# Triangle inverse by doubling in an RWKV-7 layer: 32 instead of 64 moving columns in each product, as a strided view

## The chip, the cores and the metric

One Trainium2 chip, of which the kernel uses one core. The metric is the device time of one execution in microseconds (us). The engines are TensorE (PE in the rows, its weight loads PEld), VectorE (DVE), ScalarE (ACT), GpSimd (POOL) and SyncE (SP, which issues the DMAs).

## What is computed

A trunk of two residual layers on 256 frames of 2048 features, in float32. Layer 0 mixes tokens by forgetting attention, layer 1 by RWKV-7 time mixing, and each is followed by a gated ConvFFN (5632 hidden features); each part has RMS norms before and after, and shift, scale and gate from a conditioning vector (adaLN). The change is in the RWKV-7 part, whose heart is this recurrence over the frames, for 32 heads of 64 features:

```python
def step(state, inp):
    r_t, w_t, k_t, v_t, kk_t, a_t = inp
    sa = jnp.einsum('bhvk,bhk->bhv', state, kk_t)
    state = (state * w_t[:, :, None, :]
             - sa[..., None] * (kk_t * a_t)[:, :, None, :]
             + v_t[..., None] * k_t[:, :, None, :])
    y = jnp.einsum('bhvk,bhk->bhv', state, r_t)
    return state, y
```

The kernel computes it in four chunks of 64 frames. Within a chunk the values sa solve a triangular system of 64x64 with a unit diagonal, so each head and chunk needs the inverse of such a matrix.

## The kernel before

**The whole.** Activations lie feature-major in SBUF. The big weight matrices are streamed in pieces of 512 KB by SP; ScalarE rounds each piece to fp32r (`whi`, L752), VectorE forms the rest (`wlo`, L1161), and TensorE multiplies (L1783 in `slab`, L1799 and L1802 in `paired_slab`). This fills nearly the whole time before and after the stage of the change.

**The chunk laps.** The RWKV recurrence runs in `chunk_laps`: 8 laps of 2 tiles, each tile 128 partitions that hold two heads of 64 features, so 4 heads x 4 chunks = 16 matrices a lap. `chunk_laps` issues lap 0 straight, laps 1 to 6 in a hardware loop of two laps, and then lap 7 and a last half lap. Every engine has its own `chunk_lap` with the order of its work written out by hand; semaphores named in `pr_pe`, `pr_a`, `pr_v` (preparation), `sc_*` (the recurrence) and `hd_*` (the head of the next lap) tie them together. A lap does three things at once: `prep`, the matrices of its own two tiles; `turn`, the recurrence over the four chunks of the two tiles before; and `ahead`, the LoRA products, decays and norms of the two tiles after. Beside these TensorE multiplies the adaLN weights of layer 1 by the conditioning vector (`gemv`, L2028, and `adaln_sum`, L1816, whose matmuls have one moving column).

**The inverse by doubling.** `ut[q]` holds, for each head (`h`, half of the partitions), tile `p` and chunk `c`, the inverse so far twice: index 0 upper, index 1 the transpose, lower. `lnm` holds the triangle to be inverted. `masked` and the step `tb` set level 0. Then for n = 1 to 5 (`LEVELS` = 6), with blocks of 2^n columns:

- `z_mm(n)` on TensorE: for both tiles 8 matmuls, Z = lnm^T ut0, 64 moving columns, into PSUM bank 0 or 1. It waits for `ut` of the level before.
- `z_out(n)` on ScalarE: copies Z from PSUM to `zsb` (L1098), 128x256, once per tile.
- `u_mm(n)` on TensorE: for both tiles and each matrix ut1^T zsb (upper) and, below the last level, zsb^T ut1 (lower), 64 moving columns each, into banks 2 and 3. It waits for ScalarE's copy.
- `doubled(n, p)` on VectorE: writes the product into `ut` where the level's mask is one (`copy_predicated`, L1678; L1674 at the last level).

The mask of level n keeps, in the upper half, only columns whose block number (column // 2^n) is odd, and in the lower half only those with an even one, as `shape_constants` says:

```python
lower = (h // m == q // m + 1) & ((q // m) % 2 == 0)
upper = (q // m == h // m + 1) & ((h // m) % 2 == 0)
```

**The order around it.** On TensorE the pairs lie between other work: Z1, the group norm's sum (`wide`), U1, the variance sum (`compact`), Z2, `spread_out`, the LoRA products of the next lap (`loras`), U2, `adaln_sum`, Z3, `gemv`, U3, the norms of kk (`compact`), `gemv`, Z4, `kk_spread`, `gemv`, U4, `bonuses`, `gemv`, Z5, `adaln_sum`, U5. All small matmuls go through `small_mm`, so the profile has them under L1979, and they are told apart by their tiles (a row names the output, the moving and the stationary operand in this order). `zsb` is not initialised before; the VectorE steps that come first in the stage (L1538 to L1550) end in the semaphore step `pone`, for which all engines wait before lap 0.

Of the kernel before, what the change touches and what calls it, by code (L numbers as in the profile page):

```python
# [33 lines left out]
ACT = mybir.ActivationFunctionType  # L34
# [3 lines left out]
P = 128  # L38
D = 2048
S = 256  # L40
# [8 lines left out]
HD = 64  # L49
# [25 lines left out]
LEVELS = 6  # L75
# [136 lines left out]
def trunk(nc, a, out):  # L212
# [20 lines left out]
    with ctx:  # L233
# [20 lines left out]
        def take(region, name, shape, dt=F32):  # L254

            region[0] = (region[0] + 31) // 32 * 32
            t, region[0] = at(name, region[0], shape, dt)
            assert region[0] <= region[1], (name, region)
            return t
# [16 lines left out]
        hka = take(small, "hka", [P, KT])  # L276
        hw0 = take(small, "hw0", [P, 2, KT])
# [73 lines left out]
        zsb = take(r1, "zsb", [P, 2, CH, HD])  # L351
        lnm = take(r1, "lnm", [P, 2, CH, HD])
        pcum = take(r1, "pcum", [P, 2, CH, HD + 1])
        csum = take(r1, "csum", [P, 2 * CH * HD])
        keep = take(r1, "keep", [P, 2 * CH * HD])
# [3 lines left out]
        ut = [take(r2, f"ut{q}", [P, 2, CH, 2, HD]) for q in range(2)]  # L359
# [13 lines left out]
        cst = take(r1, "cst", [P, KT, 32])  # L373
# [11 lines left out]
        ps = [duo[b // 2][:, b % 2, :] for b in range(4)]  # L385
# [20 lines left out]
        def steps(name, names, first=""):  # L406
            return Steps(sem(name), names, first)
# [14 lines left out]
                     v=steps(f"out{n}_v", "gain rinv t0 t1 x0 t2 x1 t3 x2 x3"))  # L422
                for n in range(4)]
# [11 lines left out]
                   z=steps(f"up{n}_z", "zero")) for n in range(2)]  # L435
# [13 lines left out]
                      + " ".join(f"z{n}p0 z{n}p1 u{n}p0 u{n}p1" for n in range(1, LEVELS)))  # L449
        pr_a = steps("pr_a", "vt bt kt " + " ".join(f"z{n}p{p}" for n in range(1, LEVELS) for p in range(2)))  # L450
        pr_v = steps("pr_v", "ub0 arb0 lk0 ub1 arb1 lk1 ln tb "
                     + " ".join(f"u{n}p{p}" for n in range(1, LEVELS) for p in range(2)), "hka nka hw0 one keep cz cst pone")
        sc_pe = steps("sc_pe", " ".join(f"rhs{c} sa{c} m{c} y{c}" for c in range(CH - 1)) + f" rhs{CH - 1} sa{CH - 1} "
                      f"y{CH - 1} mean var vx")
        sc_a = steps("sc_a", " ".join(f"rhs{c} sa{c}" for c in range(CH)) + " y sqy sd hi")
# [21 lines left out]
        def flat(t):  # L477
            return t[:, :, :].rearrange("p a s -> p (a s)")
# [42 lines left out]
        def waited(engine):  # L521

            engine.nop(nofuse=True)

        heads = (slice(0, HD), slice(HD, P))

        def chunk_laps(engine, head, lap):


            n = ph_chunk.iters  # L530
            head(0, 0)
            lap(0, 0, turn=False)
            with engine.Fori(0, n // 2 - 1) as j:
                lap(j * 2 + 1, 1)
                lap(j * 2 + 2, 0)
            lap(n - 1, 1, ahead=False)
            lap(n, 0, prep=False, ahead=False)
# [206 lines left out]
        def _(sc):  # L744
# [307 lines left out]
            def sigmoids(i):  # L1052

                t0 = i * 2
                sc.wait_ge(*hd_pe.at("lora", i))
                for b, nm in enumerate(("sw", "sa")):
                    for p in range(2):
                        sc.activation(sig[:, b, p, :], ps[4 + b][:, p * S:p * S + S], ACT.Tanh,
                                      bias=hw0[:, b, ds(t0 + p, 1)], scale=0.5).then_inc(*hd_a.inc(f"{nm}{p}"))
# [18 lines left out]
            def chunk_lap(i, q, prep=True, turn=True, ahead=True):  # L1078
                n_ = i - 1

                def out(name, bank):

                    if turn:
                        sc.wait_ge(*sc_pe.at(name, n_))
                        sc.activation((rhs_s if name[0] == "r" else sa)[:, :, :].rearrange("p a s -> p (a s)"),
                                      bank[:, 0:2 * HD], ACT.Copy).then_inc(*sc_a.inc(name))

                def tokens_out(name, dst, b):
                    if prep:
                        sc.wait_ge(*pr_pe.at(f"{name}tok", i))  # L1090
                        sc.activation(dst[q][:, :, :, :].rearrange("p a c s -> p (a c s)"), ps[b][:, :],
                                      ACT.Copy).then_inc(*pr_a.inc(f"{name}t"))

                def z_out(n):
                    if prep:
                        for p in range(2):
                            sc.wait_ge(*pr_pe.at(f"z{n}p{p}", i))
                            sc.activation(zsb[:, p, :, :].rearrange("p c s -> p (c s)"), ps[p][:, 0:S],  # L1098
                                          ACT.Copy).then_inc(*pr_a.inc(f"z{n}p{p}"))

                def gemv_result(u):

                    if prep:
                        sc.wait_ge(gemv_used, i * (KT // 2) + 4 * (u + 1))
                        sc.activation(mfin[:, 0:512], ps[7][:, :], ACT.Copy).then_inc(gemv_out, 1)

                tokens_out("v", vtok, 1)
                out("rhs0", ps[4])
                tokens_out("b", btok, 2)
                out("sa0", ps[5])  # L1110
                tokens_out("k", ktok, 3)
                for c in range(1, CH):
                    out(f"rhs{c}", ps[4])
                    out(f"sa{c}", ps[5])
                if turn:
                    sc.wait_ge(*sc_pe.at(f"y{CH - 1}", n_))
                    sc.activation(flat(ysb), ps[6][:, :], ACT.Copy).then_inc(*sc_a.inc("y"))
                z_out(1)
                if turn:
                    sc.wait_ge(*sc_v.at("yc", n_))  # L1120
                    sc.activation(sqy[:, :, :], yc[:, :, :], ACT.Square).then_inc(*sc_a.inc("sqy"))
                    sc.wait_ge(*sc_pe.at("var", n_))
                    sc.activation(sd8[:, :], ps[5][:, 0:8], ACT.Sqrt, bias=eps[1], scale=1.0 / HD).then_inc(
                        *sc_a.inc("sd"))
                gemv_result(0)
                z_out(2)
                if ahead:
                    sigmoids(i + 1)
                z_out(3)
                if ahead:  # L1130
                    norms(i + 1, 1 - q, turn)
                z_out(4)
                if turn:
                    sc.wait_ge(*sc_v.at("o", n_))
                    sc.activation(act[:, ds(n_ * 2, 2), 0, :], yc[:, :, :], ACT.Copy).then_inc(*sc_a.inc("hi"))
                gemv_result(1)
                z_out(5)
# [17 lines left out]
        def _(v):  # L1155
# [390 lines left out]
            v.memset(cst[:, :, :], 0.0).then_inc(*pr_v.inc("cz"))  # L1546
            v.wait_ge(*pr_v.at("cz"))
            v.tensor_copy(cst[:, :, 0], cact[:, :]).then_inc(*pr_v.inc("cst"))
            v.memset(pcum[:, :, :, 0:1], 1.0).then_inc(*pr_v.inc("pone"))
            v.nop().then_inc(*sc_v.inc("first"))  # L1550

# [209 lines left out]
        def _(pe):  # L1761
# [216 lines left out]
            def small_mm(dst, lhs, rhs, start=True, stop=True):  # L1978
                return pe.matmul(dst, lhs, rhs, start=start, stop=stop, skip_group_check=True)  # L1979
# [74 lines left out]
            def chunk_lap(i, q, prep=True, turn=True, ahead=True):  # L2054
# [73 lines left out]
                def z_mm(n):  # L2128
                    if not prep:
                        return  # L2130
                    for p in range(2):
                        pe.wait_ge(*(pr_v.at("tb", i) if n == 1 else pr_v.at(f"u{n - 1}p{p}", i)))
                        waited(pe)
                        for c in range(CH):
                            for h in heads:
                                last_ = small_mm(ps[p][h, c * HD:(c + 1) * HD], lnm[h, p, c, :],
                                                 ut[q][h, p, c, 0, :])
                        last_.then_inc(*c_.inc(f"z{n}p{p}"))

                def u_mm(n):  # L2140
                    if not prep:
                        return
                    for p in range(2):
                        pe.wait_ge(*pr_a.at(f"z{n}p{p}", i))
                        waited(pe)
                        for c in range(CH):
                            for h in heads:
                                last_ = small_mm(ps[2 + p][h, c * P:c * P + HD], ut[q][h, p, c, 1, :], zsb[h, p, c, :])
                                if n < LEVELS - 1:
                                    last_ = small_mm(ps[2 + p][h, c * P + HD:(c + 1) * P], zsb[h, p, c, :],  # L2150
                                                     ut[q][h, p, c, 1, :])
                        last_.then_inc(*c_.inc(f"u{n}p{p}"))

                if prep:
# [43 lines left out]
                if prep:  # L2198
                    gemv(i, 0, 3)
                z_mm(1)  # L2200
                if turn:
                    pe.wait_ge(*sc_a.at("y", n_))
# [75 lines left out]
```

## Time and profile before

| | |
|---|---|
| Median of 3 runs | 3188.09 us (3187.14 to 3192.75) |
| The profiled execution | 3189.45 us, span from first to last instruction 3187.7 us |
| Mean granted TensorE clock | 0.948 |
| TensorE busy | 2888.0 us, 91% of the span |
| VectorE / ScalarE / GpSimd busy | 62% / 46% / 4% |
| Stage of the chunk laps | about 1790 to 2276 us |

The span is one execution as the hardware profiler recorded it. Busy time counts an engine's own instructions; a busy TensorE may still wait inside its pipeline. An fp32 matmul of the source shows as two records, each with a weight load. PEclk is the clock granted to TensorE as a share of full speed (2.4 GHz); 0.50 is 1.2 GHz.

### The profile page before, as it was taken

The page shows a single profiled execution, that of the slowest core. Times are in us where ns is not written, and L with a number is a line of the kernel's source. Part 1 is how long each engine was busy: PE and PEld are TensorE (multiplying, and loading weights), DVE is VectorE, ACT ScalarE, POOL GpSimd, SP SyncE. Part 2 cuts the span into 40 slices and gives each one's busy share as a digit, 9 for nine tenths or more (in the row PEclk, how much of TensorE's full clock was granted, in tenths as well). Part 3 has the DMA queues.
Part 4 walks back from the last instruction along what each step waited for, and adds up shares of the span by engine and source line. Part 5 has one row for each costly group of instructions (what it writes and reads, how often), then busy time and mean ns, then how long its engine had stood idle before and what let it go on. Part 6 is the DMA issues. An engine that isn't in the chain of part 4 may idle for free.

```text
span 3187.7 us, 63222 instructions
## 1 busy us (share of the span) xinstructions
PE 2888.0 (91%) x24254; PEld 2598.9 (82%) x24254; DVE 1970.8 (62%) x2557; ACT 1474.7 (46%) x2011; POOL 136.2 (4%) x160
## 2 busy tenths in 40 slices
PE   2399999899999999985999798989789999999998
PEld 2399999888888899984888677767687888889998
DVE  6877777876666666678564344444337666665434
ACT  0133333466666643348554232322236666665333
POOL 0000000100000000000000221211000000000000
PEclk8599989999999999997999899999799999999999
DMA  8787877756666578872655454444444666655553
GB/s 297 259 279 266 290 262 264 268 170 192 188 191 188 185 241 290 274 238 69 189 178 178 136 172 142 151 159 160 128 144 152 185 186 185 188 184 175 183 172 126
DMA packets 506155, 628.09 MB, mean 197 GB/s; under 512 B 26392, under 2 KB 434824, under 8 KB 505736
## 3 DMA queue, kind: packets, MB, share of 16 engines
q1 hardware_dynamic: 501952, 622.62, 60.6%
q10 hardware_dynamic: 4040, 3.07, 0.3%
q8 instruction: 131, 2.15, 0.3%
q14 instruction: 32, 0.26, 0.0%
HBM read 623.50 MB, written 2.10 MB: 196 GB/s over the span
## 4 chain that ended last, share of the span: by engine, by line
PE 76%; DVE 10%; DMA 7%; ACT 3%; issue 3%; ACTq 0%; DVEq 0%; SPq 0%
PE ps L1799 26%; PE ps L1783 21%; PE ps L1802 13%; PE ps L1979 9%; DMA raw<-in_ffn_w_out 4%; DVE macc L1182 3%; DVE wlo L1161 2%; PE ps L2028 2%; ACT whi L752 1%; PE ps L1825 1%; PE ps L1816 1%; DMA raw<-in_mod_w 1%; DVE mx L1490 1%; PE ps L1889 1%; DMA raw<-in_fox_w_in 1%
## 5 line engine op out<-in xcount | busy, mean ns | idle before, releaser
L1161 DVE TENSOR_TENSOR wlo<-raw,whi 128x1024 fp32r<-128x1024 f32 x792 | 966.6, 1228 | 721.5 <-ACT whi L752 720.5
L752 ACT ACTIVATE whi<-raw 128x1024 fp32r<-128x1024 f32 x792 | 833.0, 1059 | 939.2 <-PE ps L1802 312.9
L1799 PE MATMUL ps<-xs,whi 128*128 128x512 f32 x3328 | 1172.1, 397 | 18.7 <-DVE xs L1245 10.9
L1802 PE MATMUL ps<-xs,wlo 128*128 128x256 f32 x3328 | 935.5, 281 | 0.0
L1799 PEld LDWEIGHTS ps<-xs,whi 128*128 128x128 f32 x3328 | 627.4, 189 | 168.1 <-issue 11.6
L1783 PE MATMUL ps<-act,whi 128*128 128x256 f32 x3840 | 708.5, 287 | 38.6 <-DVE wlo L1161 38.2
L1783 PEld LDWEIGHTS ps<-act,whi 128*128 128x128 f32 x3840 | 608.3, 195 | 45.7 <-DVE wlo L1161 44.9
L1802 PEld LDWEIGHTS ps<-xs,wlo 128*128 128x128 f32 x3328 | 631.9, 190 | 0.0
L1783 PE MATMUL ps<-act,wlo 128*128 128x256 f32 x1920 | 548.7, 286 | 0.0
L1783 PEld LDWEIGHTS ps<-act,wlo 128*128 128x128 f32 x1920 | 374.2, 195 | 0.0
L1182 DVE SCALAR_TENSOR_TENSOR macc<-raw,cact,macc 128x1024 f32<-128x1024 f32 (+1 forms) x252 | 293.0, 1163 | 9.0 <-DMA raw<-in_mod_w 4.2
L1783 PE MATMUL ps<-xs,whi 128*128 128x256 f32 x1024 | 201.2, 299 | 9.2 <-DVE xs L1245 5.7
L1783 PEld LDWEIGHTS ps<-xs,whi 128*128 128x128 f32 x1024 | 172.3, 207 | 13.4 <-issue 9.8
L1783 PE MATMUL ps<-xs,wlo 128*128 128x256 f32 x512 | 151.4, 296 | 0.0
L1443 DVE SCALAR_TENSOR_TENSOR vb<-ub,col,vb 128x256 f32<-128x256 f32 x352 | 146.7, 480 | 2.4 <-ACT vb L934 2.3
L1816 PE MATMUL ps<-con,mfin 128*128 128x1 f32 x384 | 51.7, 261 | 66.1 <-DVE mfin L1182 66.1
L1816 PEld LDWEIGHTS ps<-con,mfin 128*128 128x128 f32 x384 | 50.5, 209 | 67.5 <-DVE mfin L1182 66.3
L1783 PEld LDWEIGHTS ps<-xs,wlo 128*128 128x128 f32 x512 | 105.4, 206 | 0.0
L934 ACT ACTIVATE vb<-ub,col 128x256 f32<-128x256 f32 x176 | 95.1, 588 | 4.3 <-DVE ub L1432 4.3
L1783 PE MATMUL ps<-whi,xs 128*128 128x256 f32 x512 | 94.4, 286 | 1.4 <-DVE wlo L1161 1.3
L1799 PE MATMUL ps<-xsb,whi 128*128 128x512 f32 x256 | 90.6, 399 | 2.9 <-DVE wlo L1161 2.9
L1678 DVE COPY_PREDICATED ut<-lvl,ps 128x512 f32<-128x512 int32 x64 | 46.9, 734 | 70.6 <-PE ps L1979 70.6
(258 smaller groups left out, 3052.8 us busy)
## 6 DMA issues: line engine op xcount, KB each, us to landing
raw<-in_ffn_w_in SPq DMA_DIRECT2D x352, 512.0 KB, 3.6
raw<-in_mod_w SPq DMA_DIRECT2D x288, 512.0 KB, 5.1
raw<-in_ffn_w_out SPq DMA_DIRECT2D x176, 512.0 KB, 4.7
raw<-in_fox_w_in SPq DMA_DIRECT2D x96, 512.0 KB, 5.6
raw<-in_mod_w SPq DMA_DIRECT2D x128, 384.0 KB, 4.9
raw<-in_fox_w_out SPq DMA_DIRECT2D x32, 512.0 KB, 7.2
raw<-in_rwkv_w_r SPq DMA_DIRECT2D x32, 512.0 KB, 4.2
raw<-in_rwkv_w_k SPq DMA_DIRECT2D x32, 512.0 KB, 4.1
```

The costliest lines, as they stand in the source:

```text
L752: sc.activation(whi[:, half, :, :].rearrange("p k n -> p (k n)"), slots[slot], ACT.Copy).then_inc(w_hi, 1)
L934: sc.activation(vb[:, 2 * half + m, :], ub[:, 2 * half + m, 2:S + 2], ACT.Identity, bias=col[:, ds(c + (C_CONVB + 2 * FT * n), 1)], scale= ...
L1161: v.tensor_tensor(wlo[:, half, :, :].rearrange("p k n -> p (k n)"), slots[slot], whi[:, half, :, :].rearrange("p k n -> p (k n)").bitcast( ...
L1182: v.scalar_tensor_tensor(mfin[:, 0:cols] if kt == KT - 1 else macc[:, 0:cols], slots[slot][:, 0:cols], cact[:, kt:kt + 1], macc[:, 0:cols] ...
L1443: v.scalar_tensor_tensor(vb[:, q, :], ub[:, q, tap:tap + S], col[:, ds(c, 1)], vb[:, q, :], ALU.mult, ALU.add).then_inc(*st_.inc(f"{nm}{m}"))
L1678: v.copy_predicated(ut[q][:, p, :, :, :].rearrange("p c u s -> p c (u s)"), lvl[:, n, :].bitcast(I32).unsqueeze(1).broadcast_to([P, CH, P] ...
L1783: last = pe.matmul(ps[bank][:, m * S:m * S + S], lhs, rhs, start=begin and m == 0 and h == 0, stop=end and h == 2, skip_group_check=True)
L1799: pe.matmul(ps[bank + m][:, :], whi[:, half, k, m * P:m * P + P], src[:, kt, :, :].rearrange("p u s -> p (u s)"), start=kt == 0, stop=Fals ...
L1802: last = pe.matmul(ps[bank + m][:, 0:S], wlo[:, half, k, m * P:m * P + P], src[:, kt, 0, :], start=False, stop=kt == KT - 1, skip_group_ch ...
L1816: last = pe.matmul(pmod[:, t:t + 1], mfin[:, t * P:t * P + P], ones[:, 0:1], start=True, stop=True, skip_group_check=True)
L1979: return pe.matmul(dst, lhs, rhs, start=start, stop=stop, skip_group_check=True)
L2028: last = pe.matmul(ps[7][32 * g:32 * g + 32, :], cst[:, kt, :], slots[ph_chunk.raw(k)][:, 512 * e:512 * e + 512], start=b == 0, stop=b == ...
```

## The change

Each product of levels 1 to 5 streams only those 32 of 64 columns that the level's mask keeps, through a view that takes every other block of 2^n columns: Z, ScalarE's copy and the upper product the odd blocks, the lower product the even ones. The stationary operands stay whole (64 columns), and so do the masks and VectorE's masked copies. Z's columns in even blocks are no longer written; they enter the lower product as stationary columns, whose rows of the result the mask drops, and `zsb` is set to zero once before the laps.

```diff
@@ pr_v: a first step more
-                     ... "hka nka hw0 one keep cz cst pone")
+                     ... "hka nka hw0 one keep cz cst zz pone")
@@ a view of every other block of 2^n columns
+        def blocks(ap, n, odd):
+
+            return ap.rearrange("p (b o m) -> p b o m", o=2, m=1 << n)[:, :, odd, :]
@@ ScalarE, z_out(n)
-                            sc.activation(zsb[:, p, :, :].rearrange("p c s -> p (c s)"), ps[p][:, 0:S],
-                                          ACT.Copy).then_inc(*pr_a.inc(f"z{n}p{p}"))
+                            sc.activation(blocks(zsb[:, p, :, :].rearrange("p c s -> p (c s)"), n, 1),
+                                          blocks(ps[p][:, 0:S], n, 1), ACT.Copy).then_inc(*pr_a.inc(f"z{n}p{p}"))
@@ VectorE, before the laps
             v.tensor_copy(cst[:, :, 0], cact[:, :]).then_inc(*pr_v.inc("cst"))
+            v.memset(zsb[:, :, :, :], 0.0).then_inc(*pr_v.inc("zz"))
             v.memset(pcum[:, :, :, 0:1], 1.0).then_inc(*pr_v.inc("pone"))
@@ TensorE, z_mm(n)
-                                last_ = small_mm(ps[p][h, c * HD:(c + 1) * HD], lnm[h, p, c, :],
-                                                 ut[q][h, p, c, 0, :])
+                                last_ = small_mm(blocks(ps[p][h, c * HD:(c + 1) * HD], n, 1), lnm[h, p, c, :],
+                                                 blocks(ut[q][h, p, c, 0, :], n, 1))
@@ TensorE, u_mm(n)
-                                last_ = small_mm(ps[2 + p][h, c * P:c * P + HD], ut[q][h, p, c, 1, :], zsb[h, p, c, :])
+                                last_ = small_mm(blocks(ps[2 + p][h, c * P:c * P + HD], n, 1), ut[q][h, p, c, 1, :],
+                                                 blocks(zsb[h, p, c, :], n, 1))
                                 if n < LEVELS - 1:
-                                    last_ = small_mm(ps[2 + p][h, c * P + HD:(c + 1) * P], zsb[h, p, c, :],
-                                                     ut[q][h, p, c, 1, :])
+                                    last_ = small_mm(blocks(ps[2 + p][h, c * P + HD:(c + 1) * P], n, 0), zsb[h, p, c, :],
+                                                     blocks(ut[q][h, p, c, 1, :], n, 0))
```

## Rows read from the trace of the kernel before

**Rows 1.** The page's chain that ended last, by engine and by line.

```profile
PE 76%; DVE 10%; DMA 7%; ACT 3%; issue 3%; ACTq 0%; DVEq 0%; SPq 0%
PE ps L1799 26%; PE ps L1783 21%; PE ps L1802 13%; PE ps L1979 9%; DMA raw<-in_ffn_w_out 4%; DVE macc L1182 3%; DVE wlo L1161 2%; PE ps L2028 2%; ACT whi L752 1%; PE ps L1825 1%; PE ps L1816 1%; DMA raw<-in_mod_w 1%; DVE mx L1490 1%; PE ps L1889 1%; DMA raw<-in_fox_w_in 1%
```

**Rows 2.** Windows: stretch, length, busy time by engine (records), PEclk, DMA share, GB/s.

```profile
1790.00:2276.00 486.00, 427.19 (x8000) 341.86 (x8000) 209.98 (x421) 132.37 (x295) 94.14 (x126) 0.93 0.46 151
```

**Rows 3.** Lines L1979 and L1816: records, duration in ns (min/median/max), starts, shapes.

```profile
L1979 PE MATMUL ps<-ut,lnm x1280: 218/218/367, 1825.6 to 2245.3; 64*64 64x64 f32 x183
L1979 PE MATMUL ps<-zsb,ut x1280: 218/218/366, 1827.3 to 2247.3; 64*64 64x64 f32 x183
...
L1979 PE MATMUL ps<-rr,bneg x256: 269/269/320, 1812.5 to 2210.0; 64*64 64x128 f32 x128
...
L1979 PE MATMUL ps<-con,nrb x64: 275/275/553, 1803.0 to 2189.4; 128*128 128x128 f32 x64
...
L1816 PE MATMUL ps<-con,mfin x128: 250/250/271, 1837.5 to 2246.2; 128*128 128x1 f32 x128
```

**Rows 4.** Timeline of TensorE: start, busy time, line, operands, stationary and moving shape.

```profile
1883.98 1.13 PE L1979 MATMUL ps<-con,sdb 128*128 128x128 f32 x8 [0.32 <-DVE sdb L1710]
1885.89 0.70 PE L1979 MATMUL ps<-tw,lw 96*128 96x256 f32 x2 [0.78 <-DVE yc L1713]
1886.43 0.59 PE L1979 MATMUL ps<-ta,lw 96*128 96x256 f32 x2
...
1982.76 1.09 PE L1979 MATMUL ps<-rr,bneg 64*64 64x128 f32 x16
...
2006.76 1.05 PE L1816 MATMUL ps<-con,mfin 128*128 128x1 f32 x8
2007.74 1.15 PE L1979 MATMUL ps<-ut,lnm 64*64 64x64 f32 x32
```

**Rows 5.** Groups by shape on ScalarE, 1825 to 2265: busy, mean ns, idle before.

```profile
L1098 ACT ACTIVATE zsb<-ps 128x256 f32<-128x256 f32 x80 | 30.7, 384 | 48.4 <-PE ps L1979 45.4
...
L1085 ACT ACTIVATE rhs_s<-ps 128x128 f32<-128x128 f32 x32 | 8.8, 276 | 72.4 <-PE ps L1979 72.4
```

**Rows 6.** Timeline of the steps before lap 0, 1788 to 1791.

```profile
1788.84 0.48 DVE L1546 MEMSET cst<- 128x512 f32 x1
...
1789.49 0.07 DVE L1549 MEMSET pcum<- 128x8 f32 x1
...
1790.12 0.67 PE L1979 MATMUL ps<-tw,lw 96*128 96x256 f32 x2 [4.04 <-DMA lw<-in_rwkv_g]
```

**Rows 7.** Windows of stretches inside the laps, columns as in rows 2.

```profile
1876.40:1930.60 54.20, 50.20 (x1000) 40.18 (x1001) 26.66 (x53) 16.51 (x37) 11.89 (x16) 1.00 0.50 166
1883.60:1887.00 3.40, 2.30 (x16) 1.98 (x14) 0.92 (x2) 0.44 (x2) 1.09 (x1) 1.00 0.00 0
1890.90:1894.20 3.30, 2.84 (x67) 2.62 (x61) 3.27 (x6) 2.46 (x7) 1.62 (x3) 1.00 0.02 5
2006.50:2009.80 3.30, 2.39 (x51) 2.17 (x47) 3.27 (x8) 2.02 (x6) 2.09 (x3) 1.00 0.00 0
2009.90:2013.20 3.30, 3.27 (x34) 1.64 (x36) 2.36 (x2) 0.88 (x2) 1.54 (x2) 0.50 0.04 4
2245.40:2248.70 3.30, 2.58 (x52) 2.32 (x48) 0.94 (x3) 0.42 (x2) 0.00 (x0) 1.00 0.96 307
2248.80:2262.30 13.50, 10.86 (x170) 10.10 (x172) 2.26 (x10) 1.59 (x6) 0.00 (x0) 0.50 0.24 80
```

**Rows 8.** Timeline of ScalarE: the copy of y (L1117), once a lap, in four laps.

```profile
1876.35 0.60 ACT L1117 ACTIVATE ysb<-ps 128x512 f32<-128x512 f32 x1 [1.73 <-PE ps L1979]
...
1930.62 0.60 ACT L1117 ACTIVATE ysb<-ps 128x512 f32<-128x512 f32 x1 [1.73 <-PE ps L1979]
...
1991.18 0.60 ACT L1117 ACTIVATE ysb<-ps 128x512 f32<-128x512 f32 x1 [1.73 <-PE ps L1979]
...
2046.96 0.60 ACT L1117 ACTIVATE ysb<-ps 128x512 f32<-128x512 f32 x1 [1.73 <-PE ps L1979]
```

More of the change, by code:

```diff
@@ L451, in trunk @@
         pr_v = steps("pr_v", "ub0 arb0 lk0 ub1 arb1 lk1 ln tb "
-                     + " ".join(f"u{n}p{p}" for n in range(1, LEVELS) for p in range(2)), "hka nka hw0 one keep cz cst pone")
+                     + " ".join(f"u{n}p{p}" for n in range(1, LEVELS) for p in range(2)), "hka nka hw0 one keep cz cst zz pone")
         sc_pe = steps("sc_pe", " ".join(f"rhs{c} sa{c} m{c} y{c}" for c in range(CH - 1)) + f" rhs{CH - 1} sa{CH - 1} "
```

## The prediction

> **What bounds the kernel now.** I began with the page's busy times and its chain [rows 1]. TensorE holds 76% of the chain that ended last, and the two weight-stream lines L1799 and L1783 lead it. The changed matmuls come under L1979, with 9%. So the gain can only come from the stage of the chunk laps, and the next view shows its size: 486 us, with TensorE busy 427.19 us, VectorE 209.98 and ScalarE 132.37 [rows 2]. TensorE is the bound of this stage, with about 59 us of idle time. In the view of the line [rows 3] the records that the edit shortens stand out: 1280 of `ps<-ut,lnm` (Z) and 1280 of `ps<-zsb,ut` (the upper product of U); the lower product has 1024, as the last level lacks it. One matmul in the source leaves two records, because it is fp32: 8 laps x 5 levels x 16 matmuls x 2 = 1280.
>
> The question is what a 64x64 record waits for: its moving columns or its stationary ones. The pace answers it. In a group of N records the pace is the busy time less one record, divided by N - 1. Eight records with 128 stationary columns and 1 moving column took 1.05 us at 250 ns each: (1.05 - 0.25) / 7 = 114 ns. Eight with 128 stationary and 128 moving columns took 1.13 us at 275 ns: 122 ns [rows 3, 4]. So 127 moving columns cost 8 ns: with 128 weights, the weight load sets the pace. Where the moving side is wider than the stationary one, the stream sets it: sixteen 64x128 records took 1.09 us at 269 ns, 55 ns each. That is less than a record's own stream can take, so two records, those of the two heads on their halves of the partitions, run side by side: 109 ns per pair. 51 ns more of latency for 64 more columns (269 against 218) gives 0.80 ns a column, 102 ns for 128. A Z group of thirty-two 64x64 records took 1.15 us at 218 ns: 30 ns each, 60 per pair [rows 3, 4]. The stream of 64 columns would need 0.80 x 64 = 51 ns, and half the load of 128 weights is 114 / 2 = 57 ns. The pair's 60 ns lies nearer to the load.
>
> **The change, part by part.**
> 1. *Moving columns 64 to 32* in 3584 records. The stationary operand is unchanged at 64 columns, so by the rows above the pace stays at the weight load. Lower bound of the gain: 0. Upper bound: if the stream were all of the pace, 30 becomes 15 ns and 3584 x 15 = 54 us would go. I take 0, because the 128x1 records are nearest: they say that columns under the load are free. What does shrink is the latency of a group's last record, by 32 x 0.80 = 26 ns. It is paid only where TensorE itself waits for an answer, about three times a lap: 8 x 3 x 0.026 = -0.6 us.
> 2. *ScalarE's copy of Z* goes from 128x256 to 128x128. Such a copy from PSUM took 384 ns; the 128x128 copies at L1085 took 276 [rows 5]. 80 x 108 ns = 8.6 us of ScalarE, an engine busy for 27% of the stage. Between Z and U, TensorE has other work nearly everywhere (the group-norm sum, the LoRA products, gemv, `adaln_sum`), which took 1 us or more and hides the copies. Only lap 0 lacks it, at level 1: at most 2 x 0.1 = -0.2 us. If that cover were gone everywhere, the copies would be worth 40 x 0.2 = 8 us.
> 3. *The strided view.* No row shows a run of two elements in PSUM or SBUF. A streaming time per column that doubles makes 64 columns of 32, hidden under the load as today: 0. Four times is the far bound; it would cost 16 us (worked out with the rivals). No gain: the view reads nothing that the row does not read now. I take 0, since even a doubling costs nothing.
> 4. *The memset of zsb*, 128x512, once, ahead of `pone`: the like memset took 0.48 us. TensorE's first LoRA matmul started at 1790.12, released by a DMA, while the last memset ended at 1789.56 [rows 6]. The memset fits into those 0.56 us; POOL starts 0.48 later, and its first product is not needed for 6 us. 0, at most +0.5. No DMA is added and no wait.
> 5. VectorE's masked copies (L1678) keep their 128x512 shape. 0.
>
> Sum without the clock: -1 us.
>
> **The clock is the term that decides.** Each row of windows carries the granted clock [rows 7]. It was 1.00 (2.4 GHz) from 1876.4 to 1930.6, and 0.50 (1.2 GHz) from 2009.9 to 2013.2 and from 2248.8 to 2262.3. Before these two falls TensorE was busy for 72% and 78% of the time (2.39 of 3.30, 2.58 of 3.30). Yet from 1883.6 to 1887.0 it was busy for only 68% (2.30 of 3.40), and the clock held. Busy share does not tell them apart. Streamed columns do. The stretch that held had eight records of 128 columns and four of 256 [rows 4], 2048 columns x 0.80 = 1.6 us of streaming. Before each fall there were 8 records of one column and at most 43 or 44 of 64 columns, in pairs: 44 / 2 x 51 ns = 1.1 us. The 8 one-column records loaded weights for a whole microsecond and did not help. The stretch from 1890.9 is the same place of an earlier lap as that from 2006.5, cut a little earlier, with at most 59 records of 64, 1.5 us of streaming: the clock held [rows 7].
>
> So the laps as they are have stretches after which the clock falls and others, little fuller, after which it holds; and the change halves the streaming in just these. Three places in a lap have little but Z and U: U1, the variance sum and Z2; the end of U2, `adaln_sum` and Z3; Z5, `adaln_sum` and U5. With 8 laps that is 24 places. After 4 of them the clock falls already (those before 2009.9 and 2248.8 are two); 20 are open. What one low stretch costs can be read from the laps, which all issue the same work. From ysb to ysb (L1117) one took 54.27 us with the clock at 1.00 throughout, another 55.78 with the one low stretch from 2009.9 [rows 8]: 1.5 us.
>
> Lower bound: no new fall, 0. Upper bound: all 20 places, half of them twice as long (that from 2248.8 lasted four times as long): 20 x 1.5 x 1.5 = 45 us. I take two places in three, 13, once each: 13 x 1.5 = +20 us. Sum: 20 - 1 = +19. The profiled execution took 3189.45 us for a span of 3187.7; 3189.45 + 19 = 3208. The median of the runs shown is 3188.09, 1.4 lower, so I give 3207.
>
> The Trainium skill's page "TensorE: Matmul & The Clock Gate" (Part 1) says that the gate follows how busy the engine has been. Read with weight loads counted as busy, no fall would be added, and the sum would be -1 us; the stretch from 2245.4, busy for 78% and followed by a low clock, speaks against that reading.
>
> **The rivals.**
> - *No new falls, hence no change* (0.20). The clock may follow something else, such as matmuls issued, which the edit leaves alone. The sum is then -1, 3187, between 3184 and 3190. A strided view that reads as slowly as 64 columns ends here as well.
> - *The stream was the pace after all, faster* (0.06). For it: 60 ns a pair is not far from 51. Against it: 114 and 122 ns for 1 and 128 columns. With 15 ns off each record and four fifths of it on the path, less some falls: -54 x 0.8 + 13 = -30, 3158. The Trainium skill's page "TensorE: Matmul & The Clock Gate" (Part 1) gives a floor of about 25 ns from start to start; the estimate by it is 3584 x 5 = 18 us of gain instead of 54, and no run here shows such a floor.
> - *Strided streaming far slower than doubled, slower* (0.06). Its place is level 1, with runs of two elements: 96 records a lap, 384 pairs in all. It decides from the point where 32 columns take over 57 ns. At four times 0.80 ns the pair takes 102 instead of 60: 384 x 42 = +16 us, on top of the falls, 3223. The Trainium skill's page "SBUF — State Buffer" (the note on cachelines) warns that non-contiguous access to PSUM significantly slows matmuls; it gives no factor, and no run here shows one.
>
> **How the numbers follow.** Forecast 0.68, rivals 0.20, 0.06 and 0.06. A measurement of this kernel can tell about 0.2%, 6.4 us. Slower by more: the falls where they number over four (0.62 of the 0.68) and the strided rival, 0.68. Within: the no-fall case and few falls, 0.25. Faster: 0.07. The range goes from the no-fall case, 3185, to 3234, the upper bound of the falls (3188 + 45 - 1), and a little of the strided case; the forecast's own range is 3196 to 3234.
>
> **What would show it.** In the changed profile: Z and U groups of 32 records still near 1.1 us at the full clock, with records of about 192 ns; zsb copies near 276 ns; more stretches at 0.50 after the three places; laps of 56 to 58 us where they were 54.3. The step on pace is wrong if a Z group takes under 0.9 us. The step on the clock is wrong if the stage's mean granted clock stays near 0.93 [rows 2]; it should fall to about 0.88.

## The result and the profile after

The changed kernel took 3249.14 us in the median of its runs (3235.52 to 3272.09), against 3187.61 for the kernel before. These two medians divide to 1.0193; the ratio on record for the two kernels is 1.0221 (95% interval 1.0189 to 1.0253). The forecast was 3207 and slower; the direction came true, the time lies 15 us above the range. Run again later beside new runs of before, it gave 1.0196 (1.0128 to 1.0264), so "2%, some 62 us" is the figure to explain. The profiled execution took 3235.52 us with a span of 3233.7, 46 us above the 3187.7 of before.

First the page: busy time, and the chain, to be laid beside [rows 1]. The lines of the file have moved by 5: L1979 is now L1984, L1816 is L1821, L2028 is L2033.

```profile
PE 2942.8 (91%) x24254; PEld 2643.4 (82%) x24254; DVE 1966.9 (61%) x2558; ACT 1465.7 (45%) x2011; POOL 135.5 (4%) x160
...
PE 80%; DVE 9%; DMA 6%; ACT 3%; issue 2%; ACTq 0%; DVEq 0%; SPq 0%
PE ps L1804 26%; PE ps L1788 23%; PE ps L1807 13%; PE ps L1984 12%; DMA raw<-in_ffn_w_out 4%; DVE macc L1186 3%; PE ps L2033 3%; DVE wlo L1165 2%; ACT whi L756 1%; PE ps L1830 1%; PE ps L1821 1%; DVE mx L1494 1%; DMA raw<-in_fox_w_in 1%; PE ps L1894 1%; PE ps L1892 1%
```

The same 24254 TensorE records as before, with half the columns in 3584 of them, and TensorE is busy for 55 us longer. L1984 went from 9 to 12% of the chain. Now the stage, from its first LoRA matmul to the last `spread_out`: before (columns as in [rows 2]),

```profile
1790.10:2274.30 484.20, 426.76 (x7999) 341.72 (x8000) 208.78 (x418) 132.37 (x295) 94.04 (x125) 0.93 0.46 152
```

and after, with a whole lap and three stretches inside:

```profile
1783.50:2329.30 545.80, 496.70 (x7999) 392.90 (x8000) 206.60 (x418) 123.88 (x295) 94.30 (x128) 0.78 0.41 135
...
1883.50:1942.70 59.20, 56.01 (x1001) 44.14 (x1001) 26.43 (x53) 15.49 (x37) 11.86 (x16) 0.88 0.46 152
1898.90:1902.30 3.40, 2.18 (x45) 1.60 (x44) 3.37 (x6) 1.04 (x4) 2.93 (x3) 1.00 0.00 0
...
1902.40:1915.90 13.50, 13.50 (x134) 9.28 (x130) 5.38 (x10) 4.17 (x8) 4.64 (x5) 0.50 0.58 188
...
2274.50:2311.80 37.30, 35.42 (x440) 27.51 (x440) 9.41 (x20) 3.66 (x12) 0.00 (x0) 0.50 0.35 114
```

The stage is 61.6 us longer, which is the whole loss of the medians. (In these two profiled executions the weight streams around it happened to be 16 us shorter, hence 46 in the spans.) Its mean granted clock fell from 0.93 to 0.78. Since the traces have only two levels, 1.00 and 0.50, a mean of 0.78 over 545.8 us is 2 x 0.22 x 545.8 = 240 us at half clock, against 2 x 0.07 x 484.2 = 68 before: 172 us more. The loss is 61.6 / 172 = 0.36 us per us of low clock.

One such stretch in the timeline of TensorE, after U2 of a lap. The last rows of it, at 1916, are at full clock again:

```profile
1898.34 1.05 PE L1821 MATMUL ps<-con,mfin 128*128 128x1 f32 x8
1899.32 1.12 PE L1984 MATMUL ps<-ut,lnm 64*64 64x32 f32 x32
1901.66 1.34 PE L2033 MATMUL ps<-raw,cst 128*32 128x512 f32 x8 [1.22 <-DVE mod L1194]
...
1906.51 1.86 PE L1984 MATMUL ps<-con,sqk 128*128 128x2 f32 x8
1908.30 1.93 PE L2033 MATMUL ps<-raw,cst 128*32 128x512 f32 x8
1910.17 1.92 PE L1984 MATMUL ps<-ut,lnm 64*64 64x32 f32 x32
1912.02 2.07 PE L1984 MATMUL ps<-con,nrb 128*128 128x128 f32 x8
1914.02 1.94 PE L2033 MATMUL ps<-raw,cst 128*32 128x512 f32 x8
...
1916.05 0.28 PE L1984 MATMUL ps<-ut,zsb 64*64 64x32 f32 x4
```

A Z group of 32 records took 1.12 us at full clock, hardly less than the 1.15 of [rows 4]; the next, at half clock, took 1.92. The fall came after `adaln_sum` and Z3, one of the three thin places (where the prediction finds little but Z and U streaming), and it took with it U3, the sums of squares, two gemv pieces, Z4 and `kk_spread`: work that the edit does not touch (`con,sqk` 1.86 us, gemv 1.93). The single low stretch of the corresponding place before, 2009.9 to 2013.2 [rows 7], was over after 3.3 us.

The records of the changed matmuls, the copies of Z, and the start of the stage:

```profile
L1984 PE MATMUL ps<-ut,lnm x1280: 219/219/313, 1820.3 to 2301.7; 64*64 64x32 f32 x183
L1984 PE MATMUL ps<-zsb,ut x1280: 219/219/313, 1822.0 to 2305.3; 64*64 64x32 f32 x183
L1984 PE MATMUL ps<-ut,zsb x1024: 219/219/292, 1822.2 to 2297.9; 64*64 64x32 f32 x171
```

```profile
L1102 ACT ACTIVATE zsb<-ps 128x128 f32<-128x128 f32 x78 | 21.8, 279 | 65.2 <-PE ps L1984 64.7
```

```profile
1782.88 0.48 DVE L1553 MEMSET zsb<- 128x512 f32 x1
1783.33 0.07 DVE L1554 MEMSET pcum<- 128x8 f32 x1
...
1783.49 1.19 PE L1984 MATMUL ps<-tw,lw 96*128 96x256 f32 x2 [4.11 <-DVE pcum L1554]
```

A record of 32 columns is shown with 219 ns, no less than one of 64 (218). The copies fell from 384 to 279 ns as expected, which brings nothing: ScalarE's idle time before them, for TensorE, is 65.2 us where it was 48.4. The memset took its 0.48 us; TensorE's first LoRA matmul is now released by the last memset instead of a DMA, after 4.11 us of idle time instead of 4.04.

### The profile page after: what moved, and what is told of

It is laid out like the page before. It is cut to its first block, busy times and chain, and to the rows that moved or that the text cites. A ratio compares the mean times of both kernels' runs of the same rounds, so it can differ in the third digit from the quotient of the medians.

```text
span 3233.7 us, 63223 instructions
## 1 busy us (share of the span) xinstructions
PE 2942.8 (91%) x24254; PEld 2643.4 (82%) x24254; DVE 1966.9 (61%) x2558; ACT 1465.7 (45%) x2011; POOL 135.5 (4%) x160
## 4 chain that ended last, share of the span: by engine, by line
PE 80%; DVE 9%; DMA 6%; ACT 3%; issue 2%; ACTq 0%; DVEq 0%; SPq 0%
PE ps L1804 26%; PE ps L1788 23%; PE ps L1807 13%; PE ps L1984 12%; DMA raw<-in_ffn_w_out 4%; DVE macc L1186 3%; PE ps L2033 3%; DVE wlo L1165 2%; ACT whi L756 1%; PE ps L1830 1%; PE ps L1821 1%; DVE mx L1494 1%; DMA raw<-in_fox_w_in 1%; PE ps L1894 1%; PE ps L1892 1%
## 5 line engine op out<-in xcount | busy, mean ns | idle before, releaser
L1821 PE MATMUL ps<-con,mfin 128*128 128x1 f32 x384 | 53.3, 265 | 66.1 <-DVE mfin L1186 66.1
L1821 PEld LDWEIGHTS ps<-con,mfin 128*128 128x128 f32 x384 | 52.1, 214 | 67.2 <-DVE mfin L1186 66.3
L1984 PEld LDWEIGHTS ps<-zsb,ut 64*64 64x64 f32 x1280 | 75.4, 155 | 28.5 <-issue 28.4
L2033 PE MATMUL ps<-raw,cst 128*32 128x512 f32 x512 | 86.3, 751 | 10.9 <-DVE mod L1194 6.1
```

The costliest lines, as they stand in the source:

```text
L1821: last = pe.matmul(pmod[:, t:t + 1], mfin[:, t * P:t * P + P], ones[:, 0:1], start=True, stop=True, skip_group_check=True)
L2033: last = pe.matmul(ps[7][32 * g:32 * g + 32, :], cst[:, kt, :], slots[ph_chunk.raw(k)][:, 512 * e:512 * e + 512], start=b == 0, stop=b == ...
```

## The experiments

Two theories stood against each other. C: the loss comes from the granted clock, and the clock falls because fewer columns are streamed. S: the strided view itself (runs of 2^n columns in SBUF and PSUM) makes the matmuls slow or brings the clock down. For every run the row of its stage is shown further below. Each ratio is against runs of the kernel before that were taken beside it, and each edit is shown against the changed kernel, with lines left out where dots stand.

**All 64 columns, in strided order.** The kernel with the same views, but all columns:

```diff
+        def sorted_(ap, n):
+
+            return ap.rearrange("p (b o m) -> p o b m", o=2, m=1 << n)
...
-                                last_ = small_mm(blocks(ps[p][h, c * HD:(c + 1) * HD], n, 1), lnm[h, p, c, :],
-                                                 blocks(ut[q][h, p, c, 0, :], n, 1))
+                                last_ = small_mm(sorted_(ps[p][h, c * HD:(c + 1) * HD], n), lnm[h, p, c, :],
+                                                 sorted_(ut[q][h, p, c, 0, :], n))
...
```

> All 64 columns are streamed again, but in the order of the strided view (first the even blocks of 2^n columns, then the odd ones); ScalarE's copy is whole. Theory C (the time comes from the granted clock, which falls because fewer columns are streamed): as the kernel before, within 0.3%, some 60 us of low clock in the stage of the laps and laps of 54 to 56 us between the two that begin with a stall. Theory S (the strided view itself makes records or the clock worse): slower than before by over 1%, towards the changed kernel's 2.2%.

Measured: 1.0023 (0.9995 to 1.0052) of before. The stage took 483.9 us with a clock of 0.93 (484.2 and 0.93 before). The first Z group of a lap, whose runs have two elements:

```profile
1876.68 1.15 PE L1988 MATMUL ps<-ut,lnm 64*64 64x64 f32 x32
```

S falls: reading and writing in runs of 2, 4, 8 and 16 elements costs nothing that shows here. (At the last level the two halves in order are one run of 64.)

**32 columns in one run.**

```diff
-            return ap.rearrange("p (b o m) -> p b o m", o=2, m=1 << n)[:, :, odd, :]
+            return ap.rearrange("p (b o m) -> p b o m", o=2, m=HD // 2)[:, :, odd, :]
```

> 32 columns as in the changed kernel, but always one run of 32 (the second or first half), for every level, so the products of levels 1 to 4 are not those the inverse needs. Theory C: as the changed kernel, 1.5 to 2.7% over before, some 200 us of low clock in the stage. Theory S: most of the loss is gone, under 1% over before.

Measured: 1.0206 (1.0140 to 1.0272), stage 546.5 us, clock 0.78. The whole loss is there without any short run. The number of columns makes it, not the view.

**The copy and the memset alone.** TensorE's matmuls as before.

```diff
-                                last_ = small_mm(blocks(ps[p][h, c * HD:(c + 1) * HD], n, 1), lnm[h, p, c, :],
-                                                 blocks(ut[q][h, p, c, 0, :], n, 1))
+                                last_ = small_mm(ps[p][h, c * HD:(c + 1) * HD], lnm[h, p, c, :],
+                                                 ut[q][h, p, c, 0, :])
...
```

> TensorE as before with 64 columns, only ScalarE's copy halved and zsb set to zero. Both theories: within 0.2% of before, the copies at 279 ns instead of 384 and hidden; the memset costs nothing visible. If this is over 0.5% slower, the copy or the shifted start is part of the loss.

Measured: 1.0018 (0.9987 to 1.0049), stage 481.3 us. No loss from these two, and no gain that the runs can show. The interval is wider than the 0.2% that was named, so this only excludes a part of over 0.5%.

**Filling what is free.** If columns that stream under a weight load cost no time but count for the clock, the clock can be held with them. In the laps the matmuls with 128 stationary and 1 or 2 moving columns stream 128 instead; what reads their results takes one column of each group:

```diff
+                    if ph is ph_chunk:
+                        last = pe.matmul(pmod[:, t * P:t * P + P], mfin[:, t * P:t * P + P], ones, start=True, stop=True,
+                                         skip_group_check=True)
+                        continue
                     last = pe.matmul(pmod[:, t:t + 1], mfin[:, t * P:t * P + P], ones[:, 0:1], start=True, stop=True,
                                      skip_group_check=True)
...
-                        last = small_mm(bank[:, 4 * p + 2 * t:4 * p + 2 * t + 2], src[:, p, t * P:t * P + P], both)
+                        last = small_mm(bank[:, (2 * p + t) * P:(2 * p + t + 1) * P], src[:, p, t * P:t * P + P], blk)
```

> The changed kernel, and the matmuls with 128 stationary and 1 or 2 moving columns in the laps (adaln_sum of these laps, and the sums of squares) stream 128 columns instead, which the trace of before says fit under the weight load (114 against 122 ns a record). Theory C: these 24 to 32 records a lap add about 0.8 us of streaming to each thin place at no pace, so low clock in the stage goes down from 215 us to below 150 and the time to 0.3 to 1.5% over before. Rival (the clock follows busy time or the number of matmuls): no change against the changed kernel, 2.2% over before.

Measured: 1.0041 (1.0013 to 1.0069) where the changed kernel has 1.0221. The stage went back to 484.5 us with a clock of 0.94. In its timeline the filled group and the Z group after it:

```profile
1890.06 1.16 PE L1823 MATMUL ps<-con,mfin 128*128 128x128 f32 x8
1891.15 1.12 PE L1989 MATMUL ps<-ut,lnm 64*64 64x32 f32 x32
```

More work was given to TensorE, and the stage got 61 us back. A filled group takes 1.16 us instead of 1.05, so the filling is not quite free (0.1 us a group). A theory in which the clock follows the number of matmuls does not explain this, for the number is the same. One in which it follows busy time would have to explain it by this 0.1 us, and busy time did not tell the falls from the stretch that held in [rows 7] either. (One of the ten timed executions of this kernel took 11553 us; nothing here explains it, and no other kernel of the study did that.)

**The same filling in the kernel before.**

> The kernel before (64 columns) with the same 128-column streams under the weight loads of adaln_sum and of the sums of squares. Theory C: the three single low stretches in the laps (after 1856, 2009 and 2238 us) and part of the last ones go, at 1.5 us each; the low stretches after the stalls between loop rounds stay. Low clock in the stage from 61 us to below 45, time 0 to 0.3% under before. Rival (filling is neutral and only mended what the stride broke): same low stretches as before, same time.

Measured: 0.9970 (0.9950 to 0.9989), stage 476.1 us, clock 0.96. This is the one version that beats both kernels. The lap that held the low stretch from 2009.9 took 55.78 us from ysb to ysb before [rows 8]; here the same lap:

```profile
1983.20:2037.70 54.50, 50.78 (x1004) 40.33 (x1008) 26.54 (x53) 16.57 (x37) 11.89 (x16) 1.00 0.50 165
```

54.5 us at a clock of 1.00. Of the three single low stretches that the expectation names, those after 1856 and 2009 are gone; the one after 2238 is not:

```profile
2227.90:2231.10 3.20, 3.20 (x49) 2.20 (x41) 0.06 (x1) 0.00 (x0) 0.00 (x0) 0.50 0.24 88
```

**Z alone, U alone.** The changed kernel with one of the two products back at 64 columns.

> Only Z (1280 of the 3584 records) streams 32 columns; U streams 64. Theory C: the loss follows the streamed columns, so low clock in the stage between 80 and 160 us and 0.3 to 1.2% over before. If the loss came from U's strided writes next to each other in one bank, this would equal before.

> Only U (2304 of the 3584 records) streams 32 columns; Z streams 64. Theory C: the larger part of the loss, 0.8 to 2.0% over before, low clock in the stage 110 to 200 us. If the latency of Z's strided products were the cause, this would equal before.

Measured: Z alone 1.0021 (0.9991 to 1.0051), stage 490.2 us; U alone 1.0054 (1.0032 to 1.0076), stage 502.4. Both times are below what was expected, and Z's cannot be told from none by the runs; its stage shows 6 us and a clock of 0.91. The us at low clock lie in the ranges named, by the means of the stages 88 for Z alone and 131 for U alone. 0.21% and 0.54% do not add up to 2.2%.

**48 columns in one run.**

```diff
-            return ap.rearrange("p (b o m) -> p b o m", o=2, m=1 << n)[:, :, odd, :]
+            return ap.rearrange("p (b s) -> p b s", s=HD)[:, :, (HD // 4) * odd:(HD // 4) * (odd + 3)]
```

> 48 of 64 columns in one run, for Z, the copy and U (so the products of most levels are not those the inverse needs). Theory C: a low stretch starts where too little was streamed and holds on while the half clock halves the streaming, so the loss is not in proportion: with 3/4 of the columns it is well under half of that with 32, 0.2 to 0.9% over before, low clock in the stage 70 to 120 us. A loss in proportion to the columns left out would give 1.1%.

Measured: 1.0023 (0.9997 to 1.0048), stage 499.0 us, clock 0.89. Leaving out 16 of 64 columns, half as many as the change does, gives 0.23% of 2.2%, a tenth of the loss (by the stages 499.0 - 484.2 = 15 of 62 us, a quarter): less than the half that proportion would give.

**Filling in one kind of place.** On top of the changed kernel, the filling of `adaln_sum` alone, and that of the sums of squares alone.

> The changed kernel, only adaln_sum of the laps streams 128 columns. It stands in two of the three thin places, between U2 and Z3 and between Z5 and U5. Theory C with these places: most low stretches after them go, low clock in the stage from 235 us to 100 to 160, 0.5 to 1.3% over before. If the place of the filling does not matter, the remaining loss is in proportion to its 64 of 128 filled records' share, about 1.2 to 1.3%.

> The changed kernel, only the sums of squares (between U1 and Z2, and after U3) stream 128 columns. Theory C with these places: the low stretches that begin at U1 to Z2 and at U3 go, those after adaln_sum stay, low clock in the stage 120 to 190 us, 0.8 to 1.6% over before. e9 and e10 together bring more than the 1.8 points that both at once brought back, if one low stretch is ended or prevented by either.

> The changed kernel once more, on the chip of e9 and e10 and beside the same runs of before. All theories: 1.8 to 2.6% over before, over 200 us of low clock in the stage, with other low stretches than in its first profile.

Measured beside each other: `adaln_sum` filled 1.0072 (1.0041 to 1.0103), stage 505.9 us; sums filled 1.0106 (1.0075 to 1.0136), stage 517.9; the changed kernel 1.0196, stage 539.2. Against 1.0196 the first brings back 1.2 points and the second 0.9, together 2.1, where both at once bring 1.55 (1.0196 to 1.0041). The difference of 0.6 lies within the intervals, and the stages show none of it: 33.3 and 21.3 us, together 54.6, against 54.7 for both (539.2 - 484.5). So it is not shown that one filling ends stretches that the other would end too.

What the traces do show is that each filling acts at its own place. With `adaln_sum` filled, low stretches behind Z2 stay, and the clock then holds at 1.00 through `adaln_sum` and Z3 of two laps:

```profile
1889.60:1896.10 6.50, 5.68 (x17) 4.70 (x18) 0.69 (x1) 0.27 (x1) 1.18 (x2) 0.50 0.01 3
1896.40:1978.00 81.60, 71.34 (x1396) 56.36 (x1394) 42.74 (x82) 24.19 (x55) 19.91 (x24) 1.00 0.51 168
```

With the sums filled it is the other way round. The clock holds behind Z2 and falls at Z3, but comes back earlier, for the filled sums after U3 lie inside the low stretch:

```profile
1876.00:1892.50 16.50, 14.32 (x244) 12.59 (x240) 7.61 (x14) 5.62 (x14) 6.19 (x11) 1.00 0.28 99
1892.70:1902.70 10.00, 10.00 (x105) 6.39 (x99) 4.52 (x8) 3.09 (x5) 5.28 (x6) 0.50 0.31 107
1902.90:1913.00 10.10, 9.73 (x180) 7.30 (x178) 5.38 (x10) 2.20 (x6) 0.00 (x0) 1.00 0.94 312
```

All six stretches at Z3 of that run last about 10 us; in the profile of the changed kernel the six at Z3 last 13.5 to 17 us.

The stages of all runs. Each fence is the windows view of one kernel.

Copy and memset alone:

```profile
1799.00:2280.30 481.30, 420.23 (x7999) 335.90 (x8000) 207.94 (x418) 123.96 (x295) 94.31 (x128) 0.95 0.46 153
```

64 columns, strided:

```profile
1789.40:2273.30 483.90, 426.97 (x7999) 341.96 (x8000) 208.73 (x418) 132.18 (x295) 94.06 (x128) 0.93 0.46 152
```

32 columns in one run:

```profile
1800.40:2346.90 546.50, 499.52 (x8000) 395.07 (x8000) 206.45 (x418) 123.69 (x295) 94.38 (x128) 0.78 0.41 135
```

Z alone:

```profile
1787.10:2277.30 490.20, 437.18 (x7999) 350.18 (x8000) 210.07 (x418) 123.61 (x295) 93.68 (x128) 0.91 0.46 150
```

U alone:

```profile
1786.40:2288.80 502.40, 449.60 (x8000) 359.61 (x8000) 206.24 (x418) 124.15 (x295) 95.19 (x128) 0.87 0.44 147
```

The changed kernel, filled:

```profile
1784.90:2269.40 484.50, 428.02 (x7999) 341.55 (x8000) 207.61 (x418) 123.65 (x295) 94.34 (x128) 0.94 0.46 152
```

The kernel before, filled:

```profile
1781.40:2257.50 476.10, 422.59 (x8000) 335.85 (x8000) 207.76 (x418) 132.36 (x295) 94.06 (x125) 0.96 0.47 155
```

48 columns in one run:

```profile
1788.20:2287.20 499.00, 442.95 (x8000) 355.00 (x8000) 207.29 (x418) 128.02 (x295) 94.93 (x128) 0.89 0.45 148
```

The changed kernel, `adaln_sum` filled:

```profile
1790.80:2296.70 505.90, 453.73 (x7999) 360.61 (x8000) 206.40 (x418) 123.78 (x295) 95.48 (x128) 0.87 0.45 145
```

The changed kernel, sums filled:

```profile
1782.50:2300.40 517.90, 467.54 (x8000) 370.80 (x8000) 208.48 (x418) 123.77 (x295) 93.14 (x128) 0.84 0.43 142
```

The changed kernel again:

```profile
1785.40:2324.60 539.20, 492.65 (x7999) 389.19 (x8000) 206.00 (x418) 123.75 (x295) 94.35 (x128) 0.79 0.42 136
```

Turn each clock into us at half clock, 2 x (1 - clock) x length: from 38 us in a stage of 476.1 (filled before) over 131 us in 502.4 (U alone) to 240 in 546.5 (32 in a run). (546.5 - 476.1) / (240 - 38) = 0.35 us per us, and the kernels between lie within some 6 us of that line. The number of records is 8000 in all, DVE and ACT hardly move, and neither the stride nor the halved copy shows beside the clock.

The traces also show how the low clock is made up. The stage has 10 low stretches before, with 66.5 us in all and 6.7 on average (a stretch cut by the bounds of the stage counts with its part inside). With Z alone it has 15, of 5.8 us; with U alone 18, of 7 us; with the whole change 20, of 11.8 us, 235 us in all. So U alone nearly has the number of the changed kernel, and what it lacks is the length. Of the 20, six begin where the kernel before has six as well: three at the start of the stage, two in the pauses between loop rounds, one at the end. Six begin at or just behind Z2, six at Z3 or the gemv behind it, one at the third thin place, around Z5 and U5, and one behind the sums of squares after U3.

## Why the prediction was right and where it was wrong

- **Pace.** Right. At full clock a Z group of halved records took 1.12 us and not half of 1.15: with 64 stationary columns loaded, halving the streamed ones takes next to nothing off the pace. The rival of a faster kernel is out.
- **Latency of the last record, -0.6 us.** Wrong, though too small to matter: 32 columns show 219 ns, as 64 do. The 51 ns between 64 and 128 columns do not continue downwards.
- **Copy of Z, memset, stride.** Right, each at about 0 (copy and memset within the 0.5% of their run). The Trainium skill's page "SBUF — State Buffer" (note on cachelines) would have non-contiguous PSUM access slow the matmuls significantly; with runs of 8 to 64 bytes the run with 64 strided columns shows the same 1.15 us for a Z group and the same stage. Single elements with a stride were not tried.
- **The clock decides, and through streamed columns.** Right. The runs with 64 strided and with 32 contiguous columns separate it from the view, and filling separates it from busy time. That the gate follows how busy the engine is, as the Trainium skill's page "TensorE: Matmul & The Clock Gate" (Part 1) has it, holds here only if weight loads are left out: 8 records that load 128 weights and stream one column did not keep the clock, the same 8 with 128 columns did.
- **The size of that term.** This is the step that failed: "two places in three, 13, once each: 13 x 1.5 = +20 us". The count was near: the stage has ten low stretches more than before, though the third place has only one. (In the kernel before, the falls at 1856.3, 2009.9 and 2248.8 stand at these places; the prediction counted four.) What was mis-sized is the length of a stretch. It was taken from the kernel before, where the stretch from 2009.9 lasted 3.3 us (all ten of its stage 6.7 on average); after the change the one shown lasted 13.5 us, and the average is 11.8. The sum says the same: about 170 us more of low clock, where 13 stretches of 3.3 us would be 43. The cost of a us of low clock, 1.5 / 3.3 = 0.45, was a little too high (0.36). What was not seen is that the low clock keeps itself. At half clock the same records stream at half the rate, and the halved groups, now 1.9 us for 32 records, are again as thin as what brought the clock down; it came back only after denser work, in the timeline shown `kk_spread` and a gemv piece. The prediction had the sign of this before it (the stretch from 2248.8 that lasted 13.5 us) and used it only for half of the upper bound, 45 us.
- **The expected mean clock**, 0.88 for the stage, was 0.78 when measured; the laps, "56 to 58 us", took 59.2 in the one shown, which is the shortest; the others without a pause between loop rounds took 61.9, 62.2 and 64.4.
- **The chances.** The no-fall case and few falls add up to 0.26 (0.20 + 0.06), not 0.25; nothing hangs on it.

That a stretch lasts until denser work comes is read from the timeline, and the run with the sums filled bears it out: denser work earlier in the stretches at Z3 made them 10 instead of 13.5 to 17 us long. It agrees with the 48 columns and with Z and U alone, whose losses are far below proportion. What exactly of a matmul the clock follows is open beyond this: the runs changed the number of moving columns, not the number of partitions or the width of the weights.

## What to carry to other kernels

Before cutting moving columns, compare the stationary width: under a weight load of equal or greater width they cost next to no time in this kernel's fp32 matmuls, so halving them gained nothing. In a stage of small matmuls they may be what keeps TensorE's clock, and the loss is then paid by every matmul that follows until denser work comes. Count a low stretch by the work after the change, not by the length that such a stretch had before it. Look at the granted clock around the thin places first; where matmuls with 128 stationary columns and a handful of moving ones stand there, widening their moving side can hold the clock. It cost 0.1 us a group here and made the kernel before 0.3% faster.

## What the runs showed of the hardware beyond the expected

- 3584 matmul records cut to half their columns made TensorE busy for 55 us longer.
- Wider matmuls made the kernel faster: 128 instead of 1 or 2 columns under the same weights took 1.16 us instead of 1.05 for eight, and the stage 8 us less (484.2 to 476.1).
- A record of 32 moving fp32 columns is no shorter in the trace than one of 64 (219 and 218 ns).
- A denser group inside a low stretch shortened it: 10 us instead of 13.5 to 17 with the sums of squares after U3 filled.
- Runs of two fp32 elements, read from SBUF and written to PSUM by TensorE, went at the pace of one run of 64.
